# First attention of a two-block transformer kernel: dividing the outputs in place of the probabilities, and copying the turned probabilities with two engines

## The reference

```
s   = q @ k.T * 64 ** -0.5 + mask      # over the keys that the block sees
m   = max(s, sink)
p   = exp(s - m) / (sum(exp(s - m)) + exp(sink - m))
out = p @ v
```

## Time and profile before

| | |
|---|---|
| runs | 3358.66, 3359.58, 3361.91 us; median 3359.58 |
| profiled execution | 3360.76 us, of which the span of the profile is 3359.5 us |
| TensorE busy | 3243.2 us, 97% of the span |
| VectorE busy | 2147.4 us, 64% |
| ScalarE busy | 1390.5 us, 41% |
| first attention, scores to first matmul of the output projection | 188 to 359.5 us of the span |

### The profile page before, as it was taken

The page is one execution under the profiler, slowest core; times in us unless marked ns, Lnnn a source line. Parts: engine busy times, 40 slices in busy tenths (PEclk is TensorE's granted clock), DMA queues, the critical chain, the costliest instruction groups (busy, mean ns, idle before and its releaser), DMA issues. The chain is left out here.

```text
span 3359.5 us, 45092 instructions
## 1 busy us (share of the span) xinstructions
PE 3243.2 (97%) x17846; PEld 2766.6 (82%) x17846; DVE 2147.4 (64%) x3556; ACT 1390.5 (41%) x2242; POOL 221.6 (7%) x336
## 2 busy tenths in 40 slices
PE   7998999999999999999999999999999999999998
PEld 5787788999988888878888886789999987688887
DVE  4678467887765554568887456476777865654444
ACT  5568352333444334342223335353333443542332
POOL 0001100000010000003111000100000010010001
PEclk9999999999999999999999999999999999999999
DMA  6500114444221221225664211113333231122232
GB/s 241 201 23 2 38 67 129 132 145 138 91 94 51 97 73 55 84 75 194 201 203 173 88 46 52 38 67 116 112 104 108 86 103 57 44 88 94 94 100 76
DMA packets 98689, 334.39 MB, mean 100 GB/s; under 512 B 11872, under 2 KB 16768, under 8 KB 95024
## 3 DMA queue, kind: packets, MB, share of 16 engines
q1 hardware_dynamic: 77072, 252.63, 22.4%
q0 software_dynamic: 21408, 78.88, 7.4%
HBM read 329.37 MB, written 2.10 MB: 99 GB/s over the span
## 5 line engine op out<-in xcount | busy, mean ns | idle before, releaser
L1236 ACT ACTIVATE WH<-WR 128x1024 fp32r<-128x1024 f32 (+3 forms) x516 | 443.3, 864 | 915.4 <-PE PS L634 678.9
L1852 DVE TENSOR_TENSOR WL<-WR,WH 128x1024 fp32r<-128x1024 f32 (+3 forms) x516 | 508.2, 987 | 449.1 <-ACT WH L1236 448.0
L634 PE MATMUL PS<-HH,WH 128*128 128x512 f32 x1608 | 543.3, 372 | 12.2 <-DVE WL L1852 5.0
L634 PE MATMUL PS<-HH,WL 128*128 128x512 f32 x1608 | 538.6, 369 | 0.0
L634 PE MATMUL PS<-HL,WH 128*128 128x512 f32 x1608 | 538.1, 369 | 0.0
L634 PE MATMUL PS<-D,WH 128*128 128x512 f32 x1648 | 420.9, 360 | 0.9 <-DVE D L2305 0.8
L634 PEld LDWEIGHTS PS<-HH,WH 128*128 128x128 f32 x1608 | 279.8, 188 | 74.1 <-issue 11.0
L634 PEld LDWEIGHTS PS<-HL,WH 128*128 128x128 f32 x1608 | 278.9, 188 | 52.6 <-issue 1.0
L634 PEld LDWEIGHTS PS<-HH,WL 128*128 128x128 f32 x1608 | 279.0, 188 | 52.0
L634 PEld LDWEIGHTS PS<-D,WH 128*128 128x128 f32 x1648 | 275.6, 188 | 52.3 <-DVE D L2305 2.6
L634 PE MATMUL PS<-D,WL 128*128 128x512 f32 (+1 forms) x824 | 257.1, 360 | 0.0
(11 more groups left out here) (371 smaller groups left out, 6044.5 us busy)
## 6 DMA issues: line engine op xcount, KB each, us to landing
WR<-in_win SPq DMA_DIRECT2D x176, 512.0 KB, 3.5
AT<-in_adat POOLq DMA_DIRECT2D x144, 512.0 KB, 3.9
WR<-in_wret SPq DMA_DIRECT2D x64, 512.0 KB, 3.6
WR<-in_zin SPq DMA_DIRECT2D x36, 512.0 KB, 3.4
WR<-in_wdn SPq DMA_DIRECT2D x32, 448.0 KB, 3.4
WR<-in_wdn SPq DMA_DIRECT2D x48, 256.0 KB, 2.6
WR<-in_wdn SPq DMA_DIRECT2D x32, 320.0 KB, 3.0
AR<-in_ada SPq DMA_DIRECT2D x8, 1024.0 KB, 18.9
```

The lines of the kernel that those rows point to most:

```text
L634: mm = PE.matmul(dst[:, a:b], w(u)[:, k * P:(k + 1) * P], h[:, k, a:b], start=(k == 0 and i == 0), stop=(k == nk - 1 and i == 2))
L1236: AC.activation(M.hi(u), M.raw(u), COPY).then_inc(*on.up("w_hi", u))
L1852: VE.tensor_tensor(M.lo(u), M.raw(u), M.hi(u).bitcast(F32), ALU.subtract).then_inc(*on.up("w_lo", u))
```

## The change

The probabilities are no longer divided. VectorE takes the reciprocals of two heads at once. TensorE turns the undivided exponentials, and with every odd head two more matmuls are made: the reciprocals of each of the pair's two heads, repeated over 64 columns of weights, times the identity. This puts a tile of 128 x 128 reciprocals beside the turned head in `PS[2]`, the upper 64 rows for the even head and the lower 64 for the odd one. The odd head's copy, still by ScalarE, takes this tile along, so it is 128 columns wider. The even head's copy is made by VectorE. The values' result, now in banks 6 and 7 in turn, is multiplied with the tile of reciprocals by VectorE into `aON`, and `HH` and `HL` are made from `aON`. The events `a_turned0` and `a_turned1` are those of the even and odd heads, `o_normed` that of a pair's output.

```
@@ TensorE
-                PE.wait_ge(*on("a_prob", i))
+                PE.wait_ge(*on("a_exp", i))
...
                 if i > 0:
-                    PE.wait_ge(*on("a_turned", i - 1))
+                    PE.wait_ge(*on(f"a_turned{(i - 1) % 2}", i - 1))
+                w = len(keys(i // 16)) * P
                 for k in range(len(keys(i // 16))):
                     mm = PE.transpose(PS[2][:, k * P:(k + 1) * P], M.aP[i % 4][:, k * P:(k + 1) * P], M.aID[:, :])
+                if i % 2:
+                    PE.wait_ge(*on("a_sum", i // 2))
+                    for g in range(2):
+                        n = i % 16 - 1 + g
+                        mm = PE.matmul(PS[2][64 * g:64 * g + 64, w:w + P], M.aRSM[:, n:n + 1].to_broadcast([P, 64]), M.aID[:, :],
+                                       start=True, stop=True)
                 mm.then_inc(*on.up("a_transposed", i))
...
-                out = bank(PS, 6 + t // 4)[:, t % 4 * P:(t % 4 + 1) * P]
-                PE.wait_ge(*on("a_turned", i + 1))
+                out = bank(PS, 6 + t % 2)[:, 0:P]
+                PE.wait_ge(*on("a_turned0", i))
+                PE.wait_ge(*on("a_turned1", i + 1))
...
-                if t % 4 == 0 and b:
-                    PE.wait_ge(*on("o_lo", (b - 1, t // 4)))
+                if i > 2:
+                    PE.wait_ge(*on("o_normed", i // 2 - 2))
@@ ScalarE
-            if 0 <= i < HEADS:
-                w = len(keys(i // 16)) * P
+            if 0 <= i < HEADS and i % 2:
+                w = (len(keys(i // 16)) + 1) * P
                 AC.wait_ge(*on("a_transposed", i))
                 if i > 3:
-                    AC.wait_ge(*on("a_values", (i - 4) // 2))
-                AC.activation(M.aPT[i % 4][:, 0:w], PS[2][:, 0:w], COPY).then_inc(*on.up("a_turned", i))
+                    AC.wait_ge(*on("o_normed", (i - 4) // 2))
+                AC.activation(M.aPT[i % 4][:, 0:w], PS[2][:, 0:w], COPY).then_inc(*on.up("a_turned1", i))
...
-                    AC.wait_ge(*on("a_values", i // 2))
-                    AC.activation(HH[:, t - 3:t + 1, b * P:(b + 1) * P], bank(PS, 6 + t // 4).rearrange(
-                        "p (a b) -> p a b", b=P), COPY).then_inc(*on.up("o_hi", (b, t // 4)))
+                    AC.wait_ge(*on("o_normed", i // 2))
+                    AC.activation(HH[:, t - 3:t + 1, b * P:(b + 1) * P], M.aON[t // 4][:, :, :],
+                                  COPY).then_inc(*on.up("o_hi", (b, t // 4)))
@@ VectorE
+            i = at - LAG
+            if 0 <= i < HEADS and i % 2 == 0:
+                w = len(keys(i // 16)) * P
+                VE.wait_ge(*on("a_transposed", i))
+                if i > 3:
+                    VE.wait_ge(*on("a_values", (i - 4) // 2))
+                VE.tensor_copy(M.aPT[i % 4][:, 0:w], PS[2][:, 0:w]).then_inc(*on.up("a_turned0", i))
             i = at - 1
...
-                VE.wait_ge(*on("a_exp", i))
-                step(VE.reciprocal(M.aRSM[:, n:n + 1], M.aRSM[:, n:n + 1]), ("a_sum", i))
-                VE.tensor_scalar(M.aP[i % 4][:, 0:w], M.aP[i % 4][:, 0:w], M.aRSM[:, n:n + 1], None,
-                                 ALU.mult).then_inc(*on.up("a_prob", i))
+                if n % 2:
+                    VE.wait_ge(*on("a_exp", i))
+                    VE.reciprocal(M.aRSM[:, n - 1:n + 1], M.aRSM[:, n - 1:n + 1]).then_inc(*on.up("a_sum", i // 2))
...
+            i = at - LAG - 3
+            if 0 <= i < HEADS and i % 2 == 0:
+                b, t = i // 16, i % 16 // 2
+                w = len(keys(b)) * P
+                VE.wait_ge(*on("a_values", i // 2))
+                VE.tensor_tensor(M.aON[t // 4][:, t % 4, :], bank(PS, 6 + t % 2)[:, 0:P], M.aPT[(i + 1) % 4][:, w:w + P],
+                                 ALU.mult).then_inc(*on.up("o_normed", i // 2))
```

More of the change, by code:

```diff
@@ L344, in attention @@
         self.aP = [t(f"aP{i}", [P, NB]) for i in range(4)]
-        self.aPT = [t(f"aPT{i}", [P, 5 * P]) for i in range(4)]
+        self.aPT = [t(f"aPT{i}", [P, 6 * P]) for i in range(4)]
+        self.aON = [t(f"aON{i}", [P, 4, P]) for i in range(2)]
         self.aID = t("aID", [P, P])
@@ L1574, in attention @@
         AC.activation(M.LT[0], M.LT[1], EXP, scale=-1.0).then_inc(*on.up("decay_exp", 0))
-        for step in range(HEADS + LAG + 4):
+        for step in range(HEADS + LAG + 5):
             i = step - LAG
-            if 0 <= i < HEADS:
-                w = len(keys(i // 16)) * P
+            if 0 <= i < HEADS and i % 2:
+                w = (len(keys(i // 16)) + 1) * P
                 AC.wait_ge(*on("a_transposed", i))
                 if i > 3:
-                    AC.wait_ge(*on("a_values", (i - 4) // 2))
-                AC.activation(M.aPT[i % 4][:, 0:w], PS[2][:, 0:w], COPY).then_inc(*on.up("a_turned", i))
+                    AC.wait_ge(*on("o_normed", (i - 4) // 2))
+                AC.activation(M.aPT[i % 4][:, 0:w], PS[2][:, 0:w], COPY).then_inc(*on.up("a_turned1", i))
             i = step
@@ L1592, in attention @@
                     stack(b + 1, n // 9)
-            i = step - LAG - 3
-            if i >= 0 and i % 2 == 0:
+            i = step - LAG - 4
+            if 0 <= i < HEADS and i % 2 == 0:
                 b, t = i // 16, i % 16 // 2
                 if t % 4 == 3:
-                    AC.wait_ge(*on("a_values", i // 2))
-                    AC.activation(HH[:, t - 3:t + 1, b * P:(b + 1) * P], bank(PS, 6 + t // 4).rearrange(
-                        "p (a b) -> p a b", b=P), COPY).then_inc(*on.up("o_hi", (b, t // 4)))
+                    AC.wait_ge(*on("o_normed", i // 2))
+                    AC.activation(HH[:, t - 3:t + 1, b * P:(b + 1) * P], M.aON[t // 4][:, :, :],
+                                  COPY).then_inc(*on.up("o_hi", (b, t // 4)))
     def retention():
@@ L2391, in attention @@
         VE.wait_ge(*on("aSK", 0))
-        for at in range(HEADS + LAG + 5):
+        for at in range(HEADS + LAG + 6):
             i = at
@@ L2405, in attention @@
                 b, n = i // 16, i % 16
-                w = len(keys(b)) * P
-                VE.wait_ge(*on("a_exp", i))
-                step(VE.reciprocal(M.aRSM[:, n:n + 1], M.aRSM[:, n:n + 1]), ("a_sum", i))
-                VE.tensor_scalar(M.aP[i % 4][:, 0:w], M.aP[i % 4][:, 0:w], M.aRSM[:, n:n + 1], None,
-                                 ALU.mult).then_inc(*on.up("a_prob", i))
+                if n % 2:
+                    VE.wait_ge(*on("a_exp", i))
+                    VE.reciprocal(M.aRSM[:, n - 1:n + 1], M.aRSM[:, n - 1:n + 1]).then_inc(*on.up("a_sum", i // 2))
                 if n in (4, 9) and b < 5:
                     stack(b + 1, n // 9)
-            i = at - LAG - 4
-            if i >= 0 and i % 2 == 0:
+            i = at - LAG - 3
+            if 0 <= i < HEADS and i % 2 == 0:
+                b, t = i // 16, i % 16 // 2
[3 more added lines that the diff above has]
+                                 ALU.mult).then_inc(*on.up("o_normed", i // 2))
+            i = at - LAG - 5
+            if 0 <= i < HEADS and i % 2 == 0:
                 b, t = i // 16, i % 16 // 2
@@ L2418, in attention @@
                     VE.wait_ge(*on("o_hi", (b, t // 4)))
-                    VE.tensor_tensor(HL[:, o, b * P:(b + 1) * P], bank(PS, 6 + t // 4).rearrange("p (a b) -> p a b", b=P),
+                    VE.tensor_tensor(HL[:, o, b * P:(b + 1) * P], M.aON[t // 4][:, :, :],
                                      HH[:, o, b * P:(b + 1) * P].bitcast(F32), ALU.subtract).then_inc(*on.up("o_lo", (b, t // 4)))
```

## The result

The changed kernel takes 3381.85 us (median of 3381.32, 3382.07, 3383.81 and 3381.62) against 3359.51 before: 22.3 us or 0.66% slower; the ratio of the runs is 1.0064, with a 95% interval of 1.0051 to 1.0076. The prediction was 3380.0, from 3370 to 3391.

What follows compares the result with a forecast made beforehand. Pairs of heads were taken to be bound by TensorE's work and the wait from odd to next even turning. 22.1 us for 47 longer waits, less 2.5 relief, plus 0.8 at the end: +20.4, so 3380.0 us, range 3370 to 3391.

Steps and rivals of the forecast that it cites:

- The chain: Attention pairs: TensorE's even-head turning waits for ScalarE's copy of the odd head out of the single PS[2], at every width.
- the handover: Odd head's turning to next even head's turning: 1.62, 1.41, 1.02 us growing to 2.09, 1.88, 1.49, each +0.47, 47 times.
- Term (a): Before the added matmuls: TensorE's change from 128*128 to 128*64 leaves a gap of 0.17 us.
- Rival 1: No 0.17 us gap before the added matmuls; the handover grows by 0.30, +12.4 us in all, 3372.0; chance 0.12.
- Term (b): After the odd head's turning: the two added matmuls, four records, take 0.44 us to their end.
- rival 2: Added matmuls don't run beside each other, or VectorE's copy is late at two tiles; +10 us, 3390; chance 0.11.
- Term (c): Odd head's copy, 128 columns wider: 0.81, 0.70 and 0.49 us at five, four and two tiles.
- Rival 3: Added matmuls hidden; the handover grows by the 128 columns alone, 0.106 us; +0.4 in all, 3360.0; chance 0.07.
- The relief: VectorE's division goes, and with it disturbances of pairs: 2.5 us come back, bounds 0 and 5.4.
- The even copy: Even head's copy moves to VectorE: about 0.85 us at five tiles, 0.4 at two; worth nothing on the path.
- rival 4: Even head's copy by ScalarE holds TensorE; moving it frees 0.34 a pair, 16 us; still +6.9, 3366.5; chance 0.03.
- The end: After the last turning: added matmuls, wider copy and the product into aON add 0.8 us.

## Why the prediction was right

- *The chain.* That the odd copy binds pairs at every width is confirmed from both sides: at four and two tiles the kernel with two banks moved only this wait and gained 10.8 us, and with the reciprocals outside the handover TensorE took 0.22 us more a pair at no cost, at five tiles too.
- *Term (a),* 0.17: the gap stands before the added matmuls 46 times, and goes with the change of form though the wait stays (0.16 measured). Rival 1 falls. The Trainium skill's TensorEngine Tiling (Array Packing), Key Properties, states that going from one tiling mode to another empties the engine; this case's traces agree, with 0.17 us of idle each way between 128*128 and 128*64.
- *Term (b),* 0.44 to the end of the four records: the row says 0.44. (a) and (b) together: 0.37 forecast, 0.38 by the kernel without the matmuls. The part of rival 2 in which the two matmuls don't overlap falls.
- *Term (c):* 0.812 for 768 columns, 0.706 for 640, 0.490 for 384; 0.11 by the kernel with the narrow copy. Rival 3, in which these columns alone count, falls, since they are 0.11 of a growth of 0.49.
- *The handover:* forecast 2.09, 1.88, 1.49; measured 2.11, 1.90 to 1.94, 1.50. Over 47 handovers the sum went from 65.05 to 86.94 us, +21.9, for the 22.1 forecast; a handover's growth is 0.49 rather than 0.47, less about one us of disturbances that had stood in handovers before. The 0.02 more stands between the last added matmul and the copy: 262.03 to 262.08, 0.05 for the 0.03 forecast.
- *The relief:* forecast 2.5. Outside the handovers the pairs lost only 0.85 us (98.13 to 97.28), with that one about 1.9. In five- and four-tile blocks the disturbed pairs of 4.45, 4.01 and 3.81 became plain ones. In block 4 new ones came: two odd turnings 0.8 and 0.6 us late behind VectorE's copy. The prediction had allowed for up to two such pairs, though it also listed a turning that waits for VectorE's copy among the signs that would prove it wrong; that happened in these two pairs, for 0.9 us, and not elsewhere.
- *The even copy:* 0.82 us at five tiles and 0.42 at two, for about 0.85 and 0.4. Taking it back (3379.8) or making it alone (3366.9) shows that it wasn't on the path; rival 4 falls. What I underrated is that VectorE had little room for it in the kernel before: alone it costs 6.4 us by the medians and 7 between the turnings.
- *The end:* +0.9 for +0.8.
- *The total:* +20.5 in the span for +20.4, but with 1.6 us of chance ahead of the first turning; without these it would be 22, which is what the medians show (22.3). That the two spans agree to 0.1 us is therefore luck: the relief came out 0.6 short and the growth of the handovers 0.9 long, and the chance at the start made up for it.

## What to carry to other kernels

Two engines, neither of them full, can still set the pace together if a single buffer passes between them: TensorE and ScalarE were 94% and 80% busy in the five-tile blocks of the kernel before, and 78% and 80% in the two-tile ones. Find the pair of waits that repeats, measure it from start to start, and ask of each edit whether it lands inside that stretch; the same work beside it costs nothing. And before work is put "in a wait", follow what releases it on the other engine: with the added matmul moved to a place where it waited for VectorE, the kernel lost 65 us on the one before, three times the 22 of the change.

## What the hardware showed that I had not expected

- VectorE's reciprocal goes by the element: 0.949 us for 128x128 and 0.160 for 128x2, some 6 ns a column, while a copy that spreads the same two columns over 128 takes 0.23.
- A granted clock of 0.50 (1.2 GHz throughout) or 0.82 (part of the time at each level) in the first scores, after the same 2.4 us in which TensorE loaded no weights, moved the start of the attention by 1.15 us from one execution to another.
- The untouched 3000 us behind the attention took 2997.9 to 3004.2 us in these profiles, so a difference of 3 us between two kernels' single spans says nothing by itself; the pairs in the attention agree to 0.01.
